# Where weights are rounded, when masked groups are made, and when values and keys are prepared, in a two-block fp32 kernel

## What is computed

```python
def first_block(...):
    shift, scale, gate = split(silu(c) @ w_ada + b_ada, 3)          # the same with c_ctx for the context
    h  = rmsnorm(x, norm_g)   * (1 + scale)   + shift
    hc = rmsnorm(ctx, norm_g) * (1 + scale_c) + shift_c
    u, uc = h @ w_in, hc @ w_in
    ya = gdn_mixer(uc[:, :GDN_COLS], u[:, :GDN_COLS], ...)          # 8 heads of 128, both directions, chunked
    yb = rwkv_mixer(uc[:, GDN_COLS:], u[:, GDN_COLS:], ...)         # 16 heads of 64, both directions
    return rmsnorm(x + gate * (concat([ya, yb]) @ w_out), final_norm_g)

def gated_delta_chunked(q, k, v, beta, g, s0):                      # per chunk of 64 (GDN)
    tmat = triangular_inverse(I + lmat)
    u, wk = tmat @ (v * beta), tmat @ (kb * exp(g))
    def step(state, inp):
        v_new = u_i - wk_i @ state
        o_i = q_i @ state + attn_i @ v_new
        return state * exp(gl_i) + k_i.T @ v_new, o_i

def rwkv7_scan_step(state, r, w, k, v, kk, b):                      # per token (RWKV)
    sa = -state @ kk
    state = state * w + outer(sa, b) + outer(v, k)
    return state, state @ r

def second_block(x, c, ...):
    shift, scale, gate = split(silu(c) @ w_ada + b_ada, 3)
    h = x * (1 + scale) + shift
    q, k, v, g_attn, glu_a, glu_b, g_conv = split(h @ w_in)         # 1024, 256, 256, 1024, 1024, 1024, 1024
    y_attn = banded_sink_attention(q, k, v, rel_bias, sinks) * silu(g_attn)   # 16 heads of 64, window 128
    t = glu_a * sigmoid(glu_b)
    t = causal_depthwise_conv(t, conv_w, width=31) + conv_b
    y_conv = (silu(layer_norm(t)) @ w_pw + b_pw) * silu(g_conv)
    return layer_norm(ALPHA * x + gate * (concat([y_attn, y_conv]) @ w_out), ln_g, ln_b)
```

## Time and profile before

| | |
|---|---|
| median of 3 runs | 3928.7 us (3923.34 to 3930.75) |
| the profiled execution | 3914.84 us, span 3913.0 us |
| PE busy | 3410.2 us, 87% of the span, 19656 matmuls |
| DVE busy | 2264.5 us, 58% |
| ACT busy | 1036.2 us, 26% |
| POOL busy | 909.0 us, 23% |
| mean granted clock of TensorE | 0.944 of full speed |

### The profile page before, as it was taken

One profiled execution on the slowest core, in us unless ns is written; L12 is line 12 of the kernel. 1 busy time (PEld: TensorE's weight loads), 2 busy tenths in 40 slices (PEclk: granted clock), 3 DMA queues, 4 the chain that ended last, 5 costly groups with the idle time before them and its releaser, 6 DMA issues. The chain is left out here.

```text
span 3913.0 us, 50830 instructions
## 1 busy us (share of the span) xinstructions
PE 3410.2 (87%) x19656; PEld 2844.0 (73%) x19656; DVE 2264.5 (58%) x4083; ACT 1036.2 (26%) x1712; POOL 909.0 (23%) x707
## 2 busy tenths in 40 slices
PE   8679999989999588888888868887997988889897
PEld 1168888868888488788888867885776766677485
DVE  2544565655555467777767746775103789996323
ACT  1214555543333112122212212222002221221202
POOL 0000000000000112122212200000675665656174
PEclk9889999999999799999999969998998999999998
DMA  9122343445455445455545433322523221212232
GB/s 383 44 74 93 125 140 124 140 127 179 154 176 183 106 99 135 115 130 132 131 115 131 124 95 108 129 88 84 198 86 113 75 70 61 74 59 81 79 115 75
DMA packets 337340, 464.70 MB, mean 119 GB/s; under 512 B 189856, under 2 KB 236032, under 8 KB 330608
## 3 DMA queue, kind: packets, MB, share of 16 engines
q1 hardware_dynamic: 272576, 364.28, 30.0%
q0 software_dynamic: 26512, 83.08, 7.1%
...
## 5 line engine op out<-in xcount | busy, mean ns | idle before, releaser
L988 POOL TENSOR_TENSOR w_high<-ring_o,cst 128x1024 fp32r<-128x1024 f32 x152 | 304.3, 2002 | 427.9 <-PE pjl L1009 276.8
L990 POOL TENSOR_TENSOR w_low<-ring_o,w_high 128x1024 fp32r<-128x1024 f32 x152 | 386.8, 2545 | 11.9
L1007 PE MATMUL pjl<-high,w_high 128*128 128x512 f32 x816 | 332.0, 407 | 29.0 <-DVE low L2562 15.6
L2953 DVE SCALAR_TENSOR_TENSOR arena<-arena,par 128x512 f32<-128x512 f32 x232 | 323.2, 1393 | 7.4
L1008 PE MATMUL pjl<-low,w_high 128*128 128x512 f32 x816 | 324.5, 398 | 0.0
L1009 PE MATMUL pjl<-high,w_low 128*128 128x512 f32 x816 | 323.3, 396 | 0.0
L1992 POOL DMA_DIRECT2D arena_r<-in_w_ada x256 | 138.0, 542 | 719.1 <-DVE arena_r L2341 661.0
L1981 POOL MEMSET unused<- 128x1 f32 x3 | 0.2, 98 | 1102.3 <-POOLq L197 1102.3
L1139 DVE TENSOR_TENSOR wl_in<-ring,wh_in 128x1024 fp32r<-128x1024 f32 x136 | 164.2, 1221 | 133.5 <-ACT wh_in L1132 133.4
L1120 PE MATMUL pjl<-h_high,wh_in 128*128 128x512 f32 x544 | 214.4, 394 | 9.1 <-DVE wl_in L1139 9.1
L1120 PE MATMUL xu<-h_high,wh_in 128*128 128x512 f32 x544 | 220.6, 405 | 0.0
...
## 6 DMA issues: line engine op xcount, KB each, us to landing
ring<-in_w_lr SPq DMA_DIRECT2D x136, 512.0 KB, 4.2
arena_r<-in_w_ada POOLq DMA_DIRECT2D x256, 256.0 KB, 3.2
...
```

The costliest lines, as they stand in the source:

```text
L988: pool.tensor_tensor(h, w, one, ALU.mult).then_inc(S[done + "h"], 1)
L990: pool.tensor_tensor(l, w, h.bitcast(F32), ALU.subtract).then_inc(w_used, 1)
L1007: pe.matmul(lat, wh[:, c], ah, start=kk == 0, stop=False)
L2953: link(dve.scalar_tensor_tensor(ca[:], x[:, o:o + LAT], w[:, o:o + 1], ca[:], ALU.mult, ALU.add))
```

## The change

Three edits, in three stages.

First, in the second block's loop, POOL no longer splits the 64 halves of the loop's weights. ACT rounds them (rounded(n), called two halves ahead through ahead(t, which), and the first two before everything else in its list), and DVE subtracts (lower(n)); the calls are written in between the pieces of conv, rows, norm and gate, which are cut anew. A semaphore n_hi carries ACT's count to DVE. POOL waits until the loop's halves are used and then splits the gate columns and what follows, as before. In the body heads(1) moves from before the eighth tile's eviction to behind it.

Second, in GDN, the values and keys of the next head are prepared in slots 15 and 16 (chunk five) and no longer in 13 and 14 (chunk four).

Third, in RWKV, the masked groups LC, MB and MC come first, then BT and CT, then CV; R_GROUPS, R_STEPS, R_DONE and R_BACK get new slots (the 15 block steps in four slots and no longer three), the counts that the engines wait for follow, SP's load_a waits for the transposes, and LATER puts the w_ada rows into other slots.

```diff
--- before.py
+++ after.py
@@ -510,7 +510,7 @@
 
 
 G_TURN, G_LEFT, G_RIGHT = (3, 6, 9, 12), (4, 7, 10), (5, 8, 11)
-G_VALUES, G_KEYS = 13, 14
+G_VALUES, G_KEYS = 15, 16
 G_STEPS = {6 + n: range(3 * n, 3 * n + 3) for n in range(5)}
 G_TURNED, G_DONE = 6, 10
 G_EARLY = 11
@@ -1013,10 +1013,10 @@
 
 STEPS = 15
 LATE = 4
-LATER = {0: 1, 1: 1, 2: 2, 3: 1, 4: 1, 11: 1, 12: 1, 13: 2, 14: 1, 15: 2, 16: 2, 17: 1}
-R_GROUPS = {n: range(n - 1, n) for n in range(1, 9)} | {9: range(8, 10), 10: range(10, 12)}
-R_STEPS = {5: range(0, 5), 6: range(5, 10), 7: range(10, 15)}
-R_TURNED, R_DONE, R_BACK = 5, 7, 9
+LATER = {0: 1, 2: 1, 8: 1, 9: 1, 11: 1, 13: 2, 14: 2, 15: 1, 16: 3, 17: 3}
+R_GROUPS = {1: (0,), 2: (1,), 3: (2, 3), 4: (4, 5), 5: (6,), 6: (7,), 7: (8,), 8: (9,), 9: (10, 11), 10: ()}
+R_STEPS = {5: range(0, 4), 6: range(4, 7), 7: range(7, 11), 8: range(11, 15)}
+R_TURNED, R_DONE, R_BACK = 5, 8, 10
 
 
 def blocks_out(eng, e, S, q, a, LT, of):
@@ -1929,7 +1929,7 @@
     yT = pj[0][:, 0:LAT]
     MERGE = 3
     NT, NX = 2 * MERGE, 2 * MERGE - 2
-    GROUPS = [(name, d) for name in ("BT", "CT", "LC", "MB", "MC", "CV") for d in range(2)]
+    GROUPS = [(name, d) for name in ("LC", "MB", "MC", "BT", "CT", "CV") for d in range(2)]
 
     def diag(view, h):
 
@@ -2023,17 +2023,17 @@
             sp.dma_start(bmask, io["base16"]).then_inc(S["r_b16"], 16)
             blocks_there(0)
             blocks_back(0)
-            sp.wait_ge(S["r_q"], 6)
+            sp.wait_ge(S["r_p"], 6)
             load_a(0, 1)
             for i in range(PAIRS - 1):
                 blocks_there(i * 2 + 1)
                 blocks_back(i * 2 + 1)
-                sp.wait_ge(S["r_q"], i * 16 + 14)
+                sp.wait_ge(S["r_p"], i * 12 + 12)
                 load_a(i + 1, 0)
                 blocks_there(i * 2 + 2)
                 load_rest(i)
                 blocks_back(i * 2 + 2)
-                sp.wait_ge(S["r_q"], i * 16 + 22)
+                sp.wait_ge(S["r_p"], i * 12 + 18)
                 load_a(i + 1, 1)
             blocks_there(2 * PAIRS - 1)
             load_rest(PAIRS - 1)
@@ -2056,10 +2056,10 @@
                 name, d = GROUPS[n]
                 if n < 2:
                     pe.wait_ge(S["r_pa"], a * 2 + 2)
-                elif n < 6:
-                    pe.wait_ge(S["r_pe"], a * 4 + n - 1)
+                elif n < 8:
+                    pe.wait_ge(S["r_pd"], a * 8 + n - 1)
                 else:
-                    pe.wait_ge(S["r_pd"], a * 8 + n - 5)
+                    pe.wait_ge(S["r_pe"], a * 4 + n - 7)
                 if name == "MB" and d == 0:
                     set_there(pe, a)
                 for u in range(NL[hh] if name in ("MB", "MC") else UN):
@@ -2190,7 +2190,7 @@
 
                 name, d = GROUPS[n]
                 if name in ("BT", "CT"):
-                    act.wait_ge(S["r_p"], a * 6 + 2 + n + 1)
+                    act.wait_ge(S["r_p"], a * 6 + 2 + n - 6 + 1)
                     act.activation((BT[hh] if name == "BT" else CT)[:, d], tp[:, d], ACT.Copy).then_inc(S["r_pe"], 1)
 
             def prepare(a, hh, n):
@@ -2287,7 +2287,7 @@
                 name, d = GROUPS[n]
                 if name in ("BT", "CT"):
                     return
-                dve.wait_ge(S["r_q"], a * 8 + n - 4 + 1)
+                dve.wait_ge(S["r_q"], a * 8 + (n if n < 6 else n - 4) + 1)
                 if name == "CV":
                     dve.tensor_tensor(CV[hh][:, d], tp[:, d, :, 0:64], eg[hh][:, d].unsqueeze(2).to_broadcast([P, UN, 64]), ALU.mult).then_inc(S["r_pd"], 1)
                 else:
@@ -2625,7 +2625,9 @@
                 pool.memset(unused[:, n:n + 1], 0.0).then_inc(S[name], 1)
             pool.memset(unused[:, 7:8], 0.0).then_inc(S["z_r"], 2)
             pool.memset(unused[:, 8:9], 0.0).then_inc(S["n_done"], DONE)
-            split_weights(pool, e, "n_done", loads(half), 0, A + 4 * BODY + 16 + EARLY)
+            pool.memset(unused[:, 9:10], 0.0).then_inc(S["n_doneh"], 4 * BODY)
+            pool.wait_ge(w_used, half + 4 * BODY)
+            split_weights(pool, e, "n_done", loads(half_g), 4 * BODY, 16 + EARLY)
 
             split_weights(pool, e, "n_done", loads(half_p) + 2 * 16, A + 4 * BODY + 16 + EARLY, 2 * KT - EARLY)
 
@@ -2791,6 +2793,9 @@
         @block.scalar
         def _(act):
             P0 = pj[0][:, 0:LAT]
+            for n in range(2):
+                act.wait_ge(w_loaded[n], loads(half) + 16)
+                act.activation(e["parts"][0][:, n], ring[:, n].rearrange("p k c -> p (k c)"), ACT.Copy).then_inc(S["n_hi"], 1)
             for j in range(2):
                 for g in (2 * j, 2 * j + 1):
                     a = 64 * (g % 2)
@@ -2803,6 +2808,18 @@
                 act.activation(V[:, :, j * P:j * P + P], tp8[:, j, 0:4], ACT.Copy).then_inc(S["n_kv"], 1)
             act.wait_ge(S["n_dup"], 64)
             act.wait_ge(S["n_kv"], 6)
+            def rounded(n):
+
+                act.wait_ge(w_loaded[n % RING], loads(half) + 16 + n // RING * 16)
+                if n >= 2:
+                    act.wait_ge(S["n_done"], DONE + n - 1)
+                act.activation(e["parts"][0][:, n % 2], ring[:, n % RING].rearrange("p k c -> p (k c)"), ACT.Copy).then_inc(S["n_hi"], 1)
+
+            def ahead(t, which):
+
+                if 2 * t + 2 + which < 4 * BODY:
+                    rounded(2 * t + 2 + which)
+
             for i in range(4):
                 hw = DONE + A + i * BODY
                 if i:
@@ -2829,39 +2846,56 @@
                     act.wait_ge(S["n_y"], 2 * i + j)
                     act.activation(at_[:, j], pj[2][:, 0:LAT], ACT.Copy).then_inc(S["n_at"], 1)
 
+                T = 8 * i
+                ahead(T, 0)
                 act.wait_ge(S["n_done"], hw + 2)
                 act.activation(qs[:, 0], P0, ACT.Copy).then_inc(S["n_ev"], 1)
+                ahead(T, 1)
+                ahead(T + 1, 0)
                 act.wait_ge(S["n_done"], hw + 4)
                 act.activation(qs[:, 1], P0, ACT.Copy).then_inc(S["n_ev"], 1)
+                ahead(T + 1, 1)
                 soft(0)
+                ahead(T + 2, 0)
                 act.wait_ge(S["n_done"], hw + 6)
                 if i:
                     act.wait_ge(S["n_u"], i * 2)
                 act.activation(ab[:], P0, ACT.Copy).then_inc(S["n_ev"], 1)
+                ahead(T + 2, 1)
                 flip(0)
                 soft(1)
+                ahead(T + 3, 0)
                 act.wait_ge(S["n_done"], hw + 8)
                 act.activation(sb_[:], P0, ACT.Sigmoid).then_inc(S["n_ev"], 1)
+                ahead(T + 3, 1)
                 flip(1)
+                ahead(T + 4, 0)
                 act.wait_ge(S["n_done"], hw + 10)
                 act.wait_ge(S["n_u"], i * 2 + 1)
                 act.activation(ab[:], P0, ACT.Copy).then_inc(S["n_ev"], 1)
+                ahead(T + 4, 1)
                 heads(0)
                 soft(2)
+                ahead(T + 5, 0)
                 act.wait_ge(S["n_done"], hw + 12)
                 act.activation(sb_[:], P0, ACT.Sigmoid).then_inc(S["n_ev"], 1)
+                ahead(T + 5, 1)
                 flip(2)
                 soft(3)
+                ahead(T + 6, 0)
                 act.wait_ge(S["n_done"], hw + 14)
                 act.wait_ge(S["n_y"], 1 + i * 2)
                 act.activation(ga[:], P0, ACT.Copy)
                 act.activation(gs[:], P0, ACT.Sigmoid).then_inc(S["n_ev"], 1)
+                ahead(T + 6, 1)
                 flip(3)
-                heads(1)
+                ahead(T + 7, 0)
                 act.wait_ge(S["n_done"], hw + 16)
                 act.wait_ge(S["n_y"], 1 + i * 2 + 1)
                 act.activation(ga[:], P0, ACT.Copy)
                 act.activation(gs[:], P0, ACT.Sigmoid).then_inc(S["n_ev"], 1)
+                ahead(T + 7, 1)
+                heads(1)
             with act.Fori(0, 4) as i:
                 for t in range(2):
                     act.wait_ge(S["n_done"], DONE + A + 4 * BODY + i * RING + 2 * t + 2)
@@ -2960,31 +2994,66 @@
                 link(dve.tensor_tensor(at_[:, j], at_[:, j], gs[:], ALU.mult))
                 dve.tensor_tensor(Y[:, i * 2 + j], at_[:, j], ga[:], ALU.mult).then_inc(S["n_y"], 1)
 
+            def lower(n):
+
+                if n < 4 * BODY:
+                    dve.wait_ge(S["n_hi"], n + 1)
+                    dve.tensor_tensor(e["parts"][1][:, n % 2], ring[:, n % RING].rearrange("p k c -> p (k c)"), e["parts"][0][:, n % 2].bitcast(F32),
+                                      ALU.subtract).then_inc(w_used, 1)
+
+            lower(0)
             for i in range(4):
-                u = 2 * i
+                u, H = 2 * i, BODY * i + 1
+
+                def left(a, b):
+                    if i:
+                        conv(u - 1, a, b)
+
+                lower(H)
+                left(0, 5)
+                lower(H + 1)
                 if i:
-                    conv(u - 1, 0, 4)
                     gate(i - 1, 1)
-                    conv(u - 1, 4, 12)
```

(38 more changed lines are left out.)

1 line of the change is left out of this document (removed).

## The result

The changed kernel takes 3906.9 us (median of five runs, 3903.8 to 3910.0). The ratio to the kernel before is 0.9945, 95% interval 0.9930 to 0.9959, so it is faster, by about 22 us. The forecast was 57 us and a range of 3838 to 3904: the direction was right, the size was not, and the range missed by 3 us.

What follows compares the result with a forecast made beforehand. VectorE, stretched by GpSimd's SBUF reads, was taken to bound the second block's loop. -68 - 9 + 20 = -57 from the profiled 3914.8 gave 3857.8; with 13.9 to the median, 3872 us, range 3838 to 3904 (8 in 10).

Steps and rivals of the forecast that it cites:

- Part one: Second block's loop: weight splitting moved off GpSimd ends the stretch of VectorE's convolution steps; -68 us, bounds -50 and -76.
- 3 us of handover: Loop: 0.05 us for each of 64 weight halves, with TensorE's wait for weights put at zero.
- a cold start: Loop: TensorE's first 4.5 us at half clock cost 2.2 us, as before.
- Part two: GDN: values and keys prepared in chunk five save 1.2 us a head for seven heads; -9 us, bounds -12 and 0.
- Part three: RWKV: masked groups first, with new step and row slots, costs +20 us; bounds -8 and +35.
- (a): RWKV: more w_ada rows ahead of the state's zeroing cost 2.7 us at a pair's end, 0.8 at its middle.
- (b): RWKV: MB, moved earlier, waits for the set loads: 2.6 us of stall in one half, 0.8 in the other.
- (c): RWKV: spread steps shrink TensorE's waits; chunk four's products start at 36.1 us (was 36.8) and 34.7 (was 34.3).
- rival 2: Loop: VectorE and ScalarE pass weights late; half the halves wait 1 us, 32 us come back: 3904; chance 0.16.
- Rival 1: RWKV: the reorder doesn't hurt; 3847 if only the stall goes, about 3830 if the burst goes too; chance 0.24.
- Rivals 3 and 4: Loop: late weights in the bad phase, 4011; or steps stay 1.39 us or like waits elsewhere, about 4020; 0.04 each.
- A table load ahead of a rounding: Loop, ScalarE's queue: a 1.28 us table load could take that much of a rounding's 3.0 us; no sum changes.

Runs made afterwards that it cites:

- e12_sets_early: The changed kernel with GpSimd's set loads for the next half issued after the second row of a half instead of the fifth: 3885.0 us, ratio 0.9899.
- e6_rows_moved: The changed kernel with only the two w_ada rows of slots 8 and 9 moved to slots 0 and 2: 3887.5 us, ratio 0.9889.
- e10_groups_only: The kernel before with the loop and GDN edits and, in RWKV, only the masked-groups-first order; block steps and w_ada rows in old slots: 3837.8 us, ratio 0.9780.

## Why the prediction was wrong in size

**Part one, -68: right, and a little more.** The step means 761 ns in the loop, and 1485 in conv(7) behind it, where POOL still splits. The body is 106.1 us against 105.9 forecast, the first roundings cost 1.9 against 2.2 (TensorE waits 6.35 us ahead of the transposes of the keys, 4.46 before), TensorE never waits for a subtraction. I had set 3 us of handover and a cold start; the one was zero and the other shorter, and with them the loop and what stands ahead of it came to -72.9.

**Part two, -9: right,** -9.8. TensorE's wait at L712 for the subtraction L915 fell from 14.3 us in sum to 2.2; L712 has 9.7 us of idle time instead for which the trace names no releaser (2.8 before).

**Part three, +20: wrong, 72 in the trace (59 to 65 by the ratios), and the bound of 35 was too narrow.** Two steps of it failed: the start of chunk four, and TensorE's clock behind the longer wait for the inverse, which the sum of part three leaves out. By its steps, us per pair, means over seven pairs:

| step | forecast | measured |
|---|---|---|
| (a) the ends, chunk five | +3.5 | +3.7 |
| (b), (c) the start of chunk four | -0.3 | +3.9, of which 2.2 are slowed transposes |
| the length of chunk four | 0 | +1.9 |
| sum | +3.2 | +9.4 |

Seven pairs make 66 us; the other 6 lie in the eighth.

(a) The rows at the ends of the halves. Forecast 2.7 and 0.8. Measured at chunk five: 14.54 us against 11.69 before, and 11.17 against 10.31, so +2.9 and +0.9. Right.

(b) The set loads. Forecast: a stall of 2.6 us at MB in one half of a pair. Measured: 18.7 us in seven, 2.7 each. Right in size; I let it take back what the spread steps give in this half, and `e12_sets_early` shows that 18 us hang on it.

(c) The start of chunk four. This step failed. I laid it at 36.1 and 34.7 us of the half; it is at 37.6 to 39.9 (35.9 in the first pair, 42.6 in the last) and at 35.2 to 41.7, mean 37.4. Before, it was at 36.0 to 36.8 (35.1 and 38.3 in the first and the last pair) and at 33.8 to 39.8, mean 35.6. Three things. The inverse's way was put at 5.8 and 6 us. That is what it takes undisturbed, 5.97, but I never asked what the new rows at slots 8 and 9 do: their loads meet the blocks, and it takes 7.0 in one half and up to 8.3 in the other (`e6_rows_moved`). The earlier trace rows could not show it: DVE isn't idle ahead of L2313 there, so their 7.2 us from turn to use are DVE's own queue and not the way of the blocks, which was hidden. My 6 us for the other half was misread too: it is 8.0 from turn to use in the kernel before, again without idle time. The blocks' turn itself was where I laid it in the first half, 27.96 against 27.7, and 1 us late in the second. And behind the now longer gap the transposes run at half clock, 1.1 us more in each half.

(d) The clock in chunk four, a term that I put at nothing. With the transposes, the low clock takes 4.0 us of a pair, 28 us over seven. The steps spread over one slot more and the longer way of the blocks let TensorE run out of work ahead of L2085, 2.1 to 7.1 us a half where it was 0.6 to 1.65.

The prediction read the queue of DVE past the moved rows, but not that of POOL: a row that is used up is a load that starts. And it priced the longer wait without the clock behind it, though it had done so for the loop in part one.

**The distance between profile and median.** I carried 13.9 us from the profiled execution to the median. The profiled execution of the changed kernel has the median's own time, 3906.9. So 14 us of the gain by medians (22) aren't in the traces (8), and the forecast of 3857.8 for the profile was 49 us off, that of the median 35. What makes the kernel before vary more, 3923 to 3933, no run here settles.

**The rivals.** The time came out near rival 2's 3904, but not by its mechanism: no weight was late. Rival 1 (the reorder doesn't hurt) is what `e10_groups_only` shows for the group order, and the reverse of what the rows' slots do. Rivals 3 and 4 are out: L3001 is never waited for, and 761 ns against 1393. A table load ahead of a rounding changed nothing that can be seen.
